# Next block's input loaded a second time in transposed layout, and normalised there by VectorE, in place of transposing it on TensorE

## What is computed

```
def rms_norm(x, w):
    y = x * rsqrt(mean(x * x, -1) + EPS)
    return y * w
h = rms_norm(x, pre_norm_w) * (1.0 + scale) + shift      # scale, shift from the conditioning vector
proj = h @ w_in                                          # 1024 -> 3080
... pooling mixer on one part, gated DeltaNet in chunks on the other ...
y = concatenate([y_a, y_b]) @ w_out
x = x + gate * rms_norm(y, post_norm_w)
```

## Time and profile before

| | |
|---|---|
| median of 3 runs | 1070.5 us (1069.0 to 1070.56) |
| the profiled execution | 1070.44 us, its span 1068.6 us |
| PE busy | 1025.7 us, 96% |
| PEld, DVE, ACT, POOL busy | 804.7, 654.9, 363.4, 216.9 us |
| mean granted TensorE clock | 0.992 |
| DMA | 196.04 MB, mean 183 GB/s |

### The profile page before, as it was taken

The page is one execution under the profiler, slowest core; times in us unless marked ns, Lnnn a source line. Parts: engine busy times, 40 slices in busy tenths (PEclk is TensorE's granted clock), DMA queues, the critical chain, the costliest instruction groups (busy, mean ns, idle before and its releaser), DMA issues.

```text
span 1068.6 us, 16923 instructions
## 1 busy us (share of the span) xinstructions
PE 1025.7 (96%) x6325; PEld 804.7 (75%) x6325; DVE 654.9 (61%) x1374; ACT 363.4 (34%) x725; POOL 216.9 (20%) x222
## 2 busy tenths in 40 slices
PE   4999989989999999999999999999999999999995
PEld 1477667877877788878877788878877888788774
DVE  2489897656356794565257884565256776456644
ACT  4366322243625511143325511233326521121211
POOL 0144345455300102231000102240000100533000
PEclk9999999999999999999999999999999999999998
DMA  8597566533857554224656553224665343222265
GB/s 340 210 345 300 196 232 230 195 121 132 312 203 274 192 184 151 82 80 167 227 176 257 197 197 120 81 99 157 250 254 201 119 158 120 96 84 97 85 242 177
DMA packets 45076, 196.04 MB, mean 183 GB/s; under 512 B 8970, under 2 KB 9738, under 8 KB 27460
## 3 DMA queue, kind: packets, MB, share of 16 engines
q1 hardware_dynamic: 44996, 194.97, 50.4%
HBM read 150.14 MB, written 44.81 MB: 182 GB/s over the span
## 4 chain that ended last, share of the span: by engine, by line
PE 64%; POOL 2%; DVE 2%; issue 2%; DVEq 0%; ACT 0%; POOLq 0%; ACTq 0%
PE acc L2103 12%; PE acc L2105 11%; PE acc L2104 11%; PE ring L2153 7%; PE acc L2140 2%; PE ring L2140 2%; PE ring L2141 2%; PE ring L2142 2%; PE acc L2142 2%; PE acc L2141 2%; PE ring L2170 1%; PE ring L2179 1%; POOL win L1912 1%; PE ring L2180 1%; PE ring L2340 1%
## 5 line engine op out<-in xcount | busy, mean ns | idle before, releaser
L2103 PE MATMUL acc<-hhi,wsl 128*128 128x512 f32 x768 | 316.6, 412 | 4.8 <-DVE y L1354 4.7
L2105 PE MATMUL acc<-hhi,wsl 128*128 128x512 f32 x768 | 301.5, 393 | 0.0
L2104 PE MATMUL acc<-hlo,wsl 128*128 128x512 f32 x768 | 301.0, 392 | 0.0
L2103 PEld LDWEIGHTS acc<-hhi,wsl 128*128 128x128 f32 x768 | 145.3, 189 | 42.7 <-issue 8.7
L2105 PEld LDWEIGHTS acc<-hhi,wsl 128*128 128x128 f32 x768 | 144.9, 189 | 31.8
L2104 PEld LDWEIGHTS acc<-hlo,wsl 128*128 128x128 f32 x768 | 145.4, 189 | 26.8 <-issue 1.4
L1238 DVE SCALAR_TENSOR_TENSOR cacc<-raw,cw,cacc 128x512 f32<-128x512 f32 x144 | 112.8, 783 | 5.1
L1875 POOL TENSOR_TENSOR wsl<-wraw,wsl 128x512 fp32r<-128x512 f32 x60 | 83.0, 1399 | 105.8 <-ACT wsl L890 105.8
L923 ACT ACTIVATE raw<-acc 128x512 f32<-128x512 f32 x48 | 28.6, 595 | 132.2 <-PE acc L2105 132.2
L1132 DVE TENSOR_TENSOR hlo<-htmp,hhi 128x512 fp32r<-128x512 f32 x32 | 22.2, 692 | 62.2 <-ACT hhi L860 61.9
L1940 POOL TENSOR_TENSOR on<-on,mhalf 128x4 f32<-128x4 f32 x16 | 23.3, 1457 | 159.8 <-DVE on L1771 159.8
(11 more groups left out here) (318 smaller groups left out, 1691.8 us busy)
## 6 DMA issues: line engine op xcount, KB each, us to landing
wsl<-kept_w SPq DMA_DIRECT2D x96, 1024.0 KB, 4.8
kept_w<-wsl SPq DMA_DIRECT2D x32, 1024.0 KB, 6.4
wraw<-in_w SPq DMA_DIRECT2D x64, 256.0 KB, 4.4
xb<-in_x SPq DMA_DIRECT2D x16, 512.0 KB, 5.7
wada<-in_w_ada SPq DMA_DIRECT2D x8, 1024.0 KB, 11.7
xres<-in_x SPq DMA_DIRECT2D x16, 512.0 KB, 5.7
out_y<-ytok SPq DMA_DIRECT2D x16, 512.0 KB, 8.0
wada<-in_w_ada SPq DMA_DIRECT2D x16, 256.0 KB, 5.5
```

Source lines behind the costliest of these rows:

```text
L2103: nc.tensor.matmul(acc[t % 2][:], w[:, 0, k], hi[:, k], start=(k == 0), stop=False)
L2104: nc.tensor.matmul(acc[t % 2][:], w[:, 0, k], lo[:, k], start=False, stop=False)
L2105: last = nc.tensor.matmul(acc[t % 2][:], w[:, 1, k], hi[:, k], start=False, stop=(k == KT - 1))
```

## The change

The host gives `x` once more as `xt`, with features on partitions and rows along the free dimension. SyncE loads it for the next block into `xtr`, which lies over `xb`, once the squares are taken (at step 20, in block 0 at step 23). The squares move from slot 14 to slot 12 and the root from slot 15 to slot 13. In slot 14 VectorE writes `dg`, the identity times the root of each row, four 128x128 blocks side by side; in slot 15 TensorE multiplies it by a matrix of ones, which puts the 512 roots along the free dimension of every partition; in slot 16 VectorE copies them out to `rxb`. In slots 17 to 24 VectorE multiplies `xtr` by `rxb`, one 128x512 tile a slot. ScalarE then reads `xtr` instead of a PSUM bank. The transposes of blocks 1 to 3 are gone; those of block 0's input stay as they are. The job of the new product is put in the list of banks, so all later jobs of the slots move on by a bank.

```diff
-FRONT = (NC - 1) * NPREP - 1
-XN_FROM = FRONT + 3
+FRONT = (NC - 2) * NPREP + 2
+RX_SLOT = FRONT + 3
+XN_FROM = FRONT + 5
+XT_TILE = 20
...
+        jobs += [("rt", 2)] if slot == RX_SLOT and it < NB - 1 else []
...
+        xtr = over("xtr", re_, 24 * KB, [P, KT, BT])
...
+        dg = over("dg", rr_, 0, [P, 4, C])
+        rxb = over("rxb", rr_, 2 * KB, [P, BT])
...
-                    xt = t - 4 - (0 if it else NQ + 2)
+                    xt = t - 4 - (0 if it else NQ)
...
+                    if t == XT_TILE + (0 if it else WS) and not last:
+                        sp.wait_ge(*xsq(it, 3))
+                        for i in range(4):
+                            sp.dma_start(xtr[:, 2 * i:2 * i + 2], a["xt"][it + 1][:, 2 * i:2 * i + 2]).then_inc(x_in.sem, 16)
...
-            act.wait_ge(*job["xf"](it, m))
+            act.wait_ge(*xn(it, m))
...
-            nc.scalar.activation(hhi[:, m], bank("xf", m)[:], ACT.Identity, bias=mod[:, m, 0:1],
-                                 scale=amul[:, m, 0:1]).then_inc(h_hi.sem, 1)
+            nc.scalar.activation(hhi[:, m], xtr[:, m], ACT.Identity, bias=mod[:, m, 0:1], scale=amul[:, m, 0:1]
+                                 ).then_inc(h_hi.sem, 1)
...
-                    if XN_FROM <= slot < XN_FROM + 4 and not last:
-                        front_xn(dve, it, (slot - XN_FROM,))
+                    if slot == RX_SLOT - 1 and not last:
+                        dve.wait_ge(*rx_f(it, 0))
+                        nc.vector.tensor_tensor(dg[:], ident[:].unsqueeze(1).to_broadcast([P, 4, C]),
+                                                rx[:].unsqueeze(2).to_broadcast([P, 4, C]), ALU.mult).then_inc(dg_f.sem, 1)
+                    if slot == RX_SLOT + 1 and not last:
+                        dve.wait_ge(*job["rt"](it, 2))
+                        nc.vector.tensor_copy(rxb[:], bank("rt", 2)[:]).then_inc(turned_f.sem, 1)
+                    if XN_FROM <= slot < XN_FROM + 8 and not last:
+                        m = slot - XN_FROM
+                        if m == 0:
+                            dve.wait_ge(*turned_f(it, 2))
+                            dve.wait_ge(*x_in(it, 1))
+                        nc.vector.tensor_tensor(xtr[:, m], xtr[:, m], rxb[:], ALU.mult).then_inc(xn.sem, 1)
...
+                    if slot == RX_SLOT and not last:
+                        bank_free(pe, it, "rt", 2, (dg_f, 0))
+                        nc.tensor.matmul(bank("rt", 2)[:], ones[:], dg[:].rearrange("p t c -> p (t c)"), start=True,
+                                         stop=True).then_inc(job["rt"].sem, 1)
...
-                    if not last:
-                        front_pe(pe, it, m)
...
+        "xt": f("x_prompt")[0].reshape(NB, BT, KT, P).transpose(0, 3, 2, 1),
```

More of the change, by code:

```diff
@@ L366, in layer_kernel @@
         xb = over("xb", re_, 24 * KB, [P, 4, DM])
+        xtr = over("xtr", re_, 24 * KB, [P, KT, BT])
         tmpa = sb("tmpa", [P, 2, BT])
-        raw = sb("raw", [P, RAW, BT + CK - 1])
+        rr_ = region("region_r", RAW * (BT + CK - 1) * 4)
+        raw = over("raw", rr_, 0, [P, RAW, BT + CK - 1])
+        dg = over("dg", rr_, 0, [P, 4, C])
+        rxb = over("rxb", rr_, 2 * KB, [P, BT])
         ru = region("region_u", 4224)
@@ L849, in front_h @@
         def front_h(act, it, m):
-            act.wait_ge(*job["xf"](it, m))
+            act.wait_ge(*xn(it, m))
             if it == 0 and m == 0:
                 act.wait_ge(gate_out, 16)
[L854 to L858, removed]
+            act.wait_ge(*h_lo(it, m - 2))
+            nc.scalar.activation(htmp[:, m % 2], xtr[:, m], ACT.Identity, bias=mod[:, m, 0:1], scale=amul[:, m, 0:1])
+            if m == 0:
                 act.wait_ge(*proj(it, OUT - 1))
-            nc.scalar.activation(hhi[:, m], bank("xf", m)[:], ACT.Identity, bias=mod[:, m, 0:1],
-                                 scale=amul[:, m, 0:1]).then_inc(h_hi.sem, 1)
+            nc.scalar.activation(hhi[:, m], xtr[:, m], ACT.Identity, bias=mod[:, m, 0:1], scale=amul[:, m, 0:1]
+                                 ).then_inc(h_hi.sem, 1)
         @block.scalar
@@ L874, in _ @@
             front_act(act, PROLOGUE)
+            act.nop().then_inc(x_in.sem, x_in.step)
             act.wait_ge(*rx_f(PROLOGUE, 0))
@@ L1077, in block_of @@
                                 act.wait_ge(*ysq(it, -1))
-                            if h == 0 and sc == NC - 2 and not last:
+                            if h == 0 and sc == NC - 3 and not last:
                                 act.wait_ge(*xsq(it, 3))
@@ L1137, in _ @@
             nc.vector.memset(cpad[:], 0.0).then_inc(s_pad, 1)
-            for ev in (hist_in, hist_out, conv_a, conv, turned_f, g_c, g_j, g_a, g_y, g_sp, g_g, g_b, g_h, g_r, g_x, gc_f, g_d, k_1, k_2, b_f, bke_f, z_f, pooled_f, ya_f,
+            for ev in (hist_in, hist_out, conv_a, conv, turned_f, dg_f, g_c, g_j, g_a, g_y, g_sp, g_g, g_b, g_h, g_r, g_x, gc_f, g_d, k_1, k_2, b_f, bke_f, z_f, pooled_f, ya_f,
                        rv_f, d_1, d_2, d_b, lt_f, mt_f, y_0, x_0, lb_f, sub_f, yx_f, y_l, x_l, w_f, r_f, ao_f, ve_f, s_f, o_f, o_n, o_s, yb_f,
@@ L1184, in _ @@
             row_copy(0)
+            dve.wait_ge(*xn(PROLOGUE, 3))
+            dve.nop().then_inc(xn.sem, 4)
             dve.wait_ge(s_vec, 80)
```

17 lines of the change are left out of this document (10 added, 7 removed).

## The result

The changed kernel takes 1065.5 us (median of 5 runs, 1062.3 to 1066.5), the kernel before 1070.6 beside it (1069.0 to 1071.3): a ratio of 0.9935, 95% interval 0.9914 to 0.9957. In a second set of runs it was 0.9941 (0.9924 to 0.9957). The change makes the kernel faster by 0.6%, some 6 us, where 13.2 us were forecast. 1065.5 us lies above the range given.

The account below looks back on a forecast made before the run. TensorE, busy for 96% of the span, was taken to bound the kernel; -11.4 + 2.6 - 4.6 - 1.6 + 1.8 = -13.2 us from 1070.4 gave 1057.2 us, with a range of 1055.0 to 1063.5 us.

Parts of the forecast that it names:

- The transposes, -11.4: TensorE, three blocks: removed transposes save 3.8 us a block, 11.4 us in all, all of it on the path.
- a new wait there: Sign against the prediction: a new wait at the output tiles, where TensorE comes 0.45 us sooner to each just-emptied accumulator.
- The product with the ones, +2.6: TensorE, slot 15: the new fp32 product takes 0.86 us to the next start; three of them add 2.6 us.
- the rival of the dear product: The ones product costs four transposes' worth, 1.8 us instead of 0.86, giving 1060.0 us; chance 0.02.
- The slot 19 waits, -4.6: 2.1 us of cover removes 1.25 us in blocks 1 and 2 and leaves some 0.6 in block 0; 4.6 us saved.
- The clock, -1.6: Block 0, 236 to 240 us: the clock drop behind the slot 19 waits goes, saving 1.6 us.
- the first of these: Rival: block 0's slot 24 wait grows to about 1.9 us and drops the clock, costing 1.6 us (1058.8); chance 0.12.
- The seventh multiplication, +1.8: VectorE, slot 23, between ylo and tile 23's gate product: uncovered, it delays TensorE 0.6 us a block, 1.8 in all.
- Loads, nothing: xtr lands at about 467 us, before VectorE comes for it at 468.5, so its loads cost nothing.
- I cost both at nothing: Block 0: SyncE's wait for the squares ahead of xtr's loads, and the raw weights queued behind, put at no cost.

Follow-up runs that it names:

- the run on the output tiles: Changed kernel with tile 28's weights split ahead of ScalarE's third h tile and output tile 2's last row tile done after the other three; ratio 0.9903 to the kernel before.
- root_early: Kernel before with only the squares in slot 12, the root in slot 13 and block 0's earlier xb loads; ratio 0.9984 to the kernel before.
- after: The changed kernel's first profile, nothing further altered; the profiled execution took 1062.3 us, the fastest of five with median 1065.5 us.
- after_third: The changed kernel unaltered, run a third time as a single execution for its profile; 1066.0 us.
- xb_late: Changed kernel with block 0's loads of the next block's xb back at steps 18 to 21; ratio 0.991 to the kernel before.
- before_third: The kernel before unaltered, run a third time as a single execution for its profile; 1071.8 us.

## Why the prediction was wrong

It gave the direction, and the terms for blocks 1 and 2 nearly; the size was wrong by half, and nearly all of that lies in block 0. The prediction's terms by the stretches of the table, and the means of the three profiles of either kernel:

| stretch | forecast | measured | of it, clock |
|---|---|---|---|
| block 0 to its fourth pooling product | 0.9 - 2.1 - 1.6 = -2.8 | -0.5 | -1.1 |
| to block 1's | 0.6 - 3.8 + 0.9 - 1.25 = -3.6 | -0.8 | +0.6 |
| to block 2's | -3.6 | -4.0 | -0.6 |
| to block 3's | 0.6 - 3.8 = -3.2 | -2.8 | 0 |
| sum | -13.2 | -8.1 | -1.1 |

The profiles say 8.1 us less from 144 us on, and 1.8 us more ahead of it, together 6.3; the timed runs say some 6. Of the 5.1 us missing behind 144 us, the transposes account for some 3.2 (11.4 - 8.2), the loads of `xb` for 1.1 (the mean wait at 166 us), slot 19 for 0.3 and the clock for 0.5; the seventh multiplication gave 0.6 back. Point by point:

*The transposes, -11.4.* **This is the step that failed, in its second half**: "All of it lies on the path: TensorE does not wait anywhere in the output tiles behind slot 24 now". It did not wait because the transposes kept it busy. The price of the instructions was right: from the start of one output tile to the next, before against after, each four gave 0.41 to 0.49 us, as the earlier trace rows had it. But in block 0 TensorE now comes earlier to the first accumulator of the second half, and ScalarE's square of it is queued behind a split of raw weights, which depends on loads and not on the transposes: 1.3 to 1.5 us back. In output tile 2 it comes to the fourth row tile about 0.3 us before the last `ylo`, in each block; here in block 0, where the step should be 0.23 us and is 0.54:

```profile
267.04 0.40 PE L2167 MATMUL ring<-wsl,yhi 128*128 128x512 f32 x1
267.58 0.50 PE L2165 MATMUL ring<-wsl,yhi 128*128 128x512 f32 x1
```

The run with the transposes back prices them at 8.2 us, and the run on the output tiles takes away all but 0.3 us of both waits. I had written that a new wait there would make the prediction wrong, and had not worked out by how much each queue was ahead.

*The product with the ones, +2.6.* Right: 0.86 us each. The rival of the dear product is out.

*The slot 19 waits, -4.6.* Right for blocks 1 and 2, where both waits are gone, though the root gave 0.89 us, not 1.25, and the product the rest. With 0.89 + 0.86 = 1.75 us of cover in place of 2.1, 0.94 us is left in block 0 instead of 0.6.

*The clock, -1.6.* Right that 236 to 240 us is at full clock: all nine profiles with 0.95 us or less in slot 19 have it (and `root_early` with 1.86), the three of before don't. But the drop came back elsewhere in two of three profiles of the changed kernel, once behind the wait in slot 24, once behind the new wait at 166 us, at 1.7 us each. I had given the first of these 0.12 and did not know of the second. On average 1.1 of the 1.6 us was thus given back.

*The seventh multiplication, +1.8.* The waits grew by 0.6 us in each block, and moving it brought them back. In block 0 it cost nothing on balance, since the time was lost again at 278 us.

*Loads, nothing.* `xtr` came in time: VectorE waited for no load, issued at 455.4 and used at 467.7. But "I cost both at nothing" spoke of the loads of `xtr` and left out those of `xb` in block 0, which the change moves two steps earlier between raw weights: 0.7 to 1.4 us at 166 us in the changed kernel's three profiles, on the path. This is a second term put at nothing without a reason.

Not settled is how much of the rest is chance: the low clock in the start, 0 to 5 us in thirteen profiles of nearly the same code, is nearly as large as the whole effect, and three profiles of either kernel can't say that the change leaves it alone.

## What to carry to other kernels

When work is taken off the busiest engine, ask of each thing it will meet next how far ahead its producer is, in every block with other loads, not only whether the engine waits there now. A stretch without waits may be a stretch with cover. In a block that also streams raw data, any load moved forward is a load moved in front of others; follow the queue of the engine that consumes them, and what stands behind that consumer. Where single executions differ by more than the effect, cut the profiles at the same instructions: the same stretches agreed within 0.1 us from block 1's product on, but for one drop of the clock, where the times of one kernel differed by up to 11 us.

## What the runs showed of the hardware

A drop of the clock cost 1.7 us (some 3.4 us at half speed) or twice that: 3.4 us at 68 to 76 us in `after`, `after_third` and `xb_late`, and around 152 us in `root_early`. It came behind waits of TensorE, but over different places the length of the wait alone does not decide. Behind 2.17 us in slot 19 of block 0 it came in three of three profiles, behind 1.86 us there (`root_early`) not, behind 1.9 to 2.0 us in slot 24 in two of seven, behind 1.3 to 1.4 us in slot 24 in none of six. Behind 1.33 to 1.36 us at 166 us, with work of 32x32 and 64x64 products around, it came in two of three, and once behind 1.26 us in slot 19 of block 2 of the kernel before (one of the six such waits of its three profiles; here `before_third`):

```profile
712.00:716.00 4.00, 3.61 (x13) 3.25 (x14) 2.51 (x5) 2.13 (x9) 0.00 (x0) 0.59 0.00 0
```

At one place the length did sort them: of the waits for `gg` near 70 us, the nine of 1.41 us and more all had low clock behind them, the four of 1.24 us and less had none.

The releaser that the profile names can be a bystander: at 278.28 us it gave GpSimd's split of another tile's weights, and VectorE's and ScalarE's rows told the real chain.
